# Weight sums of a seven-product mlp by adding DMAs, activation sums and squared ReLU on VectorE

## What is computed

```python
def squared_relu_mlp(xn, w_ff1, w_ff2):
    h = jax.nn.relu(jnp.einsum('bsd,df->bsf', xn, w_ff1))
    return jnp.einsum('bsf,fd->bsd', h * h, w_ff2)
...
        xn = rmsnorm(h, norm_mlp_g[l])
        h = h + squared_relu_mlp(xn, w_ff1[l], w_ff2[l])
    return rmsnorm(h, norm_final_g)
```

## Time and profile before

| | |
|---|---|
| median of 3 runs | 3379.59 us (3378.85 to 3383.29) |
| profiled execution | 3375.55 us, its span 3373.8 us |
| mean granted TensorE clock | 0.965 |
| PE busy over the span | 3018.7 us (89%) |
| VectorE (DVE), ScalarE (ACT), GpSimd (POOL) | 1725.5, 1108.4, 578.7 us |
| DMA | 370.07 MB, mean 110 GB/s |
| mlp | from 2696 to 3364 us of the span |

### The profile page before, as it was taken

The page is one execution under the profiler, slowest core; times in us unless marked ns, Lnnn a source line. Parts: engine busy times, 40 slices in busy tenths (PEclk is TensorE's granted clock), DMA queues, the critical chain, the costliest instruction groups (busy, mean ns, idle before and its releaser), DMA issues. The chain is left out here.

```text
span 3373.8 us, 36498 instructions
## 1 busy us (share of the span) xinstructions
PE 3018.7 (89%) x14456; PEld 2254.7 (67%) x14456; DVE 1725.5 (51%) x2218; ACT 1108.4 (33%) x1640; POOL 578.7 (17%) x375
## 2 busy tenths in 40 slices
PE   7997778999998888877874999999999989999998
PEld 7886754667776575322222877888787767777776
DVE  4126856884444344111114746531215379898988
ACT  3433335663334221100003131121222354636363
POOL 0002022110000001111112000000000055656663
PEclk9998889999999999999997999999999999999999
DMA  3111000003220038999995122211113111111111
GB/s 100 47 48 6 10 14 1 1 1 119 75 81 13 26 143 344 420 421 420 415 414 235 59 67 52 81 50 50 35 55 123 38 63 51 50 51 51 50 57 50
DMA packets 140073, 370.07 MB, mean 110 GB/s; under 512 B 45888, under 2 KB 59840, under 8 KB 113920
## 3 DMA queue, kind: packets, MB, share of 16 engines
q1 hardware_dynamic: 129552, 346.97, 28.3%
q0 software_dynamic: 9216, 16.80, 1.3%
q10 hardware_dynamic: 1152, 4.19, 0.3%
HBM read 352.70 MB, written 32.83 MB: 114 GB/s over the span
## 5 line engine op out<-in xcount | busy, mean ns | idle before, releaser
L4351 PE MATMUL mlp_ps<-mlp_w_ring,mlp_a_ring 128*128 128x512 f32 x1344 | 316.3, 397 | 18.3 <-issue 13.1
L4351 PE MATMUL mlp_ps<-mlp_a_ring,mlp_w_ring 128*128 128x512 f32 x1344 | 313.1, 393 | 21.2 <-issue 13.9
L4285 POOL TENSOR_TENSOR mlp_raw<-mlp_raw 128x1024 f32<-128x1024 f32 x64 | 178.6, 2797 | 892.0 <-POOLq L572 671.0
L4351 PEld LDWEIGHTS mlp_ps<-mlp_w_ring,mlp_a_ring 128*128 128x128 f32 x1344 | 257.9, 193 | 76.1 <-issue 21.9
L4351 PEld LDWEIGHTS mlp_ps<-mlp_a_ring,mlp_w_ring 128*128 128x128 f32 x1344 | 253.0, 189 | 79.0 <-issue 24.1
L517 DVE TENSOR_TENSOR m_w_cut<-m_w_raw,m_w_cut 128x512 fp32r<-128x512 f32 (+1 forms) x86 | 80.8, 940 | 414.0 <-ACT m_w_cut L513 413.6
L2963 PE MATMUL ffn_ps<-moe_wgu,moe_rowsT 128*64 128x512 f32 x1024 | 243.0, 630 | 51.5 <-issue 25.9
L513 ACT ACTIVATE m_w_cut<-m_w_raw 128x512 fp32r<-128x512 f32 (+1 forms) x86 | 71.4, 830 | 490.4 <-PE m_gates_ps L626 190.7
L2999 DVE TENSOR_TENSOR moe_hid<-ffn_ps,moe_gated 128x256 f32<-128x256 f32 x32 | 13.6, 425 | 414.3 <-ACT moe_gated L3011 414.3
L4241 DVE TENSOR_TENSOR mlp_w_ring<-mlp_raw,mlp_w_ring 128x1024 fp32r<-128x1024 f32 x112 | 219.6, 1961 | 0.0
L2963 PEld LDWEIGHTS ffn_ps<-moe_wgu,moe_rowsT 128*64 128x64 f32 x1024 | 78.7, 145 | 195.2 <-issue 166.7
(11 more groups left out here) (575 smaller groups left out, 6457.0 us busy)
## 6 DMA issues: line engine op xcount, KB each, us to landing
moe_wgu<-in_moe_w_gate_dram SPq DMA_DIRECT2D x64, 1024.0 KB, 19.3
moe_wgu<-in_moe_w_up_dram SPq DMA_DIRECT2D x64, 1024.0 KB, 24.6
moe_wd<-in_moe_w_down_dram SPq DMA_DIRECT2D x64, 1024.0 KB, 25.5
mlp_raw<-in_w_ff_dram SPq DMA_DIRECT2D x64, 512.0 KB, 6.5
m_w_raw<-in_w_in_dram SPq DMA_DIRECT2D x48, 256.0 KB, 2.8
mix_w_raw<-in_w_in_dram SPq DMA_DIRECT2D x40, 256.0 KB, 2.6
m_w_raw<-in_w_in_dram SPq DMA_DIRECT2D x20, 512.0 KB, 3.7
x_w_raw<-in_x_w_kv_dram SPq DMA_DIRECT2D x16, 512.0 KB, 3.6
```

The costliest lines, as they stand in the source:

```text
L4285: nc.gpsimd.tensor_tensor(out, l, r, ALU.add if name == "S1" else ALU.subtract).then_inc(self.summed, 1)
L4351: ins = self.nc.tensor.matmul(self.ps[:, 4 * banks + tile], l, r, start=(opens and h == k == n == 0), stop=(h == k == 1 and n == 2), skip_ ...
```

## The change

GpSimd no longer computes. The schemes' signs are turned so that each T is a sum with plus signs only: T1 = B11 + B12, T2 = B22 + B11 + B12, T4 = T2 + B21, T3 = B22 + B12. The products of index 3, 4 and 5 come out negative and are subtracted (or copied with scale -1) when they are taken. B22 is loaded twice, into slots 2 and 3, and 10 DMAs a unit of 512 KB, issued on GpSimd's queue with an add, put the other quarters on top: B11, B12 and later B21 on slot 2, B12 on slot 0 (over B11, when its split is done) and on slot 3. A second set of semaphores (`more`) counts them. The first four of unit 0 are issued in m2_out's block (`tail.gpsimd`), where that block's GpSimd part gets a call. S1 to S4 are VectorE instructions after the low parts of pieces 1, 2, 3, 4, 6 and 7 of the unit. The squared ReLU is one VectorE instruction, max(x, 0) times x, behind the adds of the product that completes the block. ScalarE's two go.

```diff
@@ project: GpSimd's part of the block
                 if side:
                     side.gpsimd(pool)
+                if tail:
+                    tail.gpsimd(pool)
...
+NEGATIVE = (3, 4, 5)
+SUMS = (("S1", 0), ("S2", 0), ("S1", 1), ("S2", 1), ("S4", 0), ("S4", 1), ("S3", 0), ("S3", 1))
+SUMS_AT = {1: SUMS[0:2], 2: SUMS[2:4], 3: SUMS[4:5], 4: SUMS[5:6], 6: SUMS[6:7], 7: SUMS[7:8]}
...
-SLOTS = {"B11": 0, "B21": 1, "B12": 2, "B22": 3, "T1": 0, "T2": 4, "T3": 2, "T4": 4}
+SLOTS = {"B11": (0, 1), "T1": (0, 2), "B21": (1, 1), "T2": (2, 3), "T4": (2, 4), "B22": (3, 1), "T3": (3, 2)}
+MORE = (1, 0, 3, 1)
...
+    def filled(self, eng, u, slot, h, times):
+        if times == 1:
+            eng.wait_ge(self.arrived[slot][h], 16 * (u + 1))
+        else:
+            eng.wait_ge(self.more[slot][h], 16 * (MORE[slot] * u + times - 1))
...
+    def load_more(self, pool, u, name, slot, h):
+        pool.dma_start(self.raw[:, slot, 2 * h:2 * h + 2], self.block_of(u, name, h),
+                       accum_op=ALU.add).then_inc(self.more[slot][h], 16)
@@ high_w
-        if name[0] == "B":
-            act.wait_ge(self.arrived[SLOTS[name]][h], 16 * (u + 1))
-        else:
-            act.wait_ge(self.summed, self.sum_done(u, name, h))
+        self.filled(act, u, SLOTS[name][0], h, SLOTS[name][1])
@@ sum
+    def sum(self, dve, u, name, h):
+        nc, out = self.nc, self.a_sum(name, h)
+        if name == "S1":
...
+            ins = nc.vector.tensor_tensor(out, self.a_block(u, "A22", h), self.a_block(u, "A21", h), ALU.subtract)
+        elif name == "S2":
...
+            ins = nc.vector.scalar_tensor_tensor(out, self.a_sum("S1", h), -1.0, self.a_block(u, "A11", h),
+                                                 ALU.mult, ALU.subtract)
+        elif name == "S4":
+            dve.wait_ge(self.a_low, self.split(u, "S2", h))
+            ins = nc.vector.scalar_tensor_tensor(out, self.a_block(u, "A12", h), -1.0, self.a_sum("S2", h),
+                                                 ALU.mult, ALU.subtract)
         else:
+            dve.wait_ge(self.a_low, self.split(u, "S4", h))
+            ins = nc.vector.tensor_tensor(out, self.a_block(u, "A11", h), self.a_block(u, "A21", h), ALU.subtract)
+        ins.then_inc(self.summed, 1)
@@ take
-                    nc.scalar.activation(at, ps, ACT.Copy).then_inc(self.copied, 1)
+                    nc.scalar.activation(at, ps, ACT.Copy, scale=-1.0 if q in NEGATIVE else 1.0).then_inc(
+                        self.copied, 1)
...
-                nc.vector.tensor_tensor(at, ps, at, ALU.add).then_inc(self.added, 1)
+                nc.vector.tensor_tensor(at, at, ps, ALU.subtract if q in NEGATIVE else ALU.add).then_inc(
+                    self.added, 1)
@@ square
-            act.wait_ge(self.added, self.adds[self.at(u, q)] + 2 * h + 2)
-            self.nc.scalar.activation(at, at, ACT.Relu).then_inc(self.squared, 1)
-            act.wait_ge(self.squared, self.final_done(u, block, h))
-            self.nc.scalar.activation(at, at, ACT.Square).then_inc(self.made, 1)
+            dve.wait_ge(self.added, self.adds[self.at(u, q)] + 2 * h + 2)
+            self.nc.vector.scalar_tensor_tensor(at, at, 0.0, at, ALU.max, ALU.mult).then_inc(self.made, 1)
@@ begin
-        for name in ("B11", "B21", "B12"):
+        for name, slot in (("B22", 2), ("B11", 0), ("B21", 1)):
             for h in range(2):
-                self.load(sp, 0, name, h)
+                self.load(sp, 0, name, slot, h)
+    def first_sums(self, pool, u):
+        for name, times in (("B11", 1), ("B12", 2)):
+            for h in range(2):
+                self.filled(pool, u, 2, h, times)
+                self.load_more(pool, u, name, 2, h)
@@ run, SP
+                        if u == 0:
+                            sp.wait_ge(rows.turned, NT)
                             for h in range(2):
+                                self.load(sp, 0, "B22", 3, h)
+                            continue
+                        for name, slot, was in (("B21", 1, "B21"), ("B11", 0, "T1"), ("B22", 3, "T3"), ("B22", 2, "T4")):
+                            for h in range(2):
+                                sp.wait_ge(self.w_low, self.split(u - 1, was, h))
+                                self.load(sp, u, name, slot, h)
@@ run, GpSimd
                     for u in range(len(units)):
-                        for name, h in SUMS:
-                            self.sum(pool, u, name, h)
+                        if u:
+                            self.first_sums(pool, u)
+                        for name, slot, was in (("B12", 0, "B11"), ("B21", 2, "T2"), ("B12", 3, "B22")):
+                            for h in range(2):
+                                pool.wait_ge(self.w_low, self.split(u, was, h))
+                                self.load_more(pool, u, name, slot, h)
@@ run, VectorE
                         u, q, h = self.piece(g)
+                        for name, half in SUMS_AT.get(2 * q + h, ()):
+                            self.sum(dve, u, name, half)
                         if h:
                             self.take(dve, u, q, "vector")
+                            if units[u].up and any(not first for _, first in TAKES[q]):
+                                self.square(dve, u, q)
...
+    def gpsimd(self, pool):
+        self.sevens.first_sums(pool, 0)
```

More of the change, by code:

```diff
@@ L4140, in __init__ @@
         self.arrived = [[sem(f"slot{s}_half{h}_arrived") for h in range(2)] for s in range(4)]
+        self.more = [[sem(f"slot{s}_half{h}_more") for h in range(2)] for s in range(4)]
         self.a_high, self.a_low, self.w_high, self.w_low = [sem(n) for n in ("a_high", "a_low", "w_high", "w_low")]
-        self.summed, self.products, self.added, self.copied, self.squared, self.made = [sem(n) for n in (
-            "summed", "products", "added", "copied", "squared", "made")]
+        self.summed, self.products, self.added, self.copied, self.made = [sem(n) for n in (
+            "summed", "products", "added", "copied", "made")]
         self.adds, self.copies = [], []
@@ L4190, in c_block, with block_of, load @@
         return self.units[u].dst[:, 4 * i + tile, j * CH:(j + 1) * CH]
-    def load(self, sp, u, name, h):
+    def block_of(self, u, name, h):
         i, k = int(name[2]) - 1, int(name[1]) - 1
-        src = self.units[u].w[:, 4 * k + 2 * h:4 * k + 2 * h + 2, i * CH:(i + 1) * CH]
-        sp.dma_start(self.w_slot(name, h), src).then_inc(self.arrived[SLOTS[name]][h], 16)
+        return self.units[u].w[:, 4 * k + 2 * h:4 * k + 2 * h + 2, i * CH:(i + 1) * CH]
+    def load(self, sp, u, name, slot, h):
+        sp.dma_start(self.raw[:, slot, 2 * h:2 * h + 2], self.block_of(u, name, h)).then_inc(
+            self.arrived[slot][h], 16)
+    def load_more(self, pool, u, name, slot, h):
+        pool.dma_start(self.raw[:, slot, 2 * h:2 * h + 2], self.block_of(u, name, h),
+                       accum_op=ALU.add).then_inc(self.more[slot][h], 16)
     def act_ready(self, eng, u, name, h):
@@ new lines, in sum @@
+    def sum(self, dve, u, name, h):
+        nc, out = self.nc, self.a_sum(name, h)
+        if name == "S1":
+            self.act_ready(dve, u, "A22", h)
+            self.act_ready(dve, u, "A21", h)
+            if u:
+                dve.wait_ge(self.a_low, self.split(u - 1, "S1", h))
+            ins = nc.vector.tensor_tensor(out, self.a_block(u, "A22", h), self.a_block(u, "A21", h), ALU.subtract)
+        elif name == "S2":
+            if u:
+                dve.wait_ge(self.a_low, self.split(u - 1, "S3", h))
+            dve.wait_ge(self.summed, self.sum_done(u, "S1", h))
+            ins = nc.vector.scalar_tensor_tensor(out, self.a_sum("S1", h), -1.0, self.a_block(u, "A11", h),
+                                                 ALU.mult, ALU.subtract)
@@ L4277, in sum @@
         elif name == "S4":
-            mine("S2")
-            pool.wait_ge(self.a_low, self.split(u, "S2", h))
-            l, r = self.a_block(u, "A12", h), self.a_sum("S2", h)
-        else:
-            mine("S4")
-            pool.wait_ge(self.a_low, self.split(u, "S4", h))
-            l, r = self.a_block(u, "A11", h), self.a_block(u, "A21", h)
-        nc.gpsimd.tensor_tensor(out, l, r, ALU.add if name == "S1" else ALU.subtract).then_inc(self.summed, 1)
+            dve.wait_ge(self.a_low, self.split(u, "S2", h))
@@ L4371, in _ @@
                     for u in range(len(units)):
-                        if u:
+                        if u == 0:
+                            sp.wait_ge(rows.turned, NT)
                             for h in range(2):
-                                sp.wait_ge(self.w_low, self.split(u - 1, "T1", h))
-                                self.load(sp, u, "B11", h)
+                                self.load(sp, 0, "B22", 3, h)
+                            continue
+                        for name, slot, was in (("B21", 1, "B21"), ("B11", 0, "T1"), ("B22", 3, "T3"), ("B22", 2, "T4")):
                             for h in range(2):
```

(19 more changed lines are left out.)

39 lines of the change are left out of this document (4 added, 35 removed).

## The result

The kernel after takes 3339.32 us, the median of 4 runs (3335.91 to 3343.0); the kernel before took 3380.41 beside it (3378.85 to 3383.29). The ratio is 0.9878, 95% interval 0.9861 to 0.9895: faster by 1.2%, where 3335 us was forecast and 3328 to 3364 was the range. The profiled execution took 3335.98 us, its span 3334.2.

What follows compares the result with a forecast made beforehand. TensorE, with holes made by GpSimd's sums, was taken as the bound. The profiled 3375.55 - 49.2 (mlp) + 5 (m2_out) gave 3331.3; with the profiled run 4.0 below the median, the forecast was 3335 us, range 3328 to 3364.

Steps and rivals of the forecast that it cites:

- Unit 0, units 1 to 6, unit 7: In the mlp's eight units, closing TensorE's holes was to gain 14.2, 27.3 and 7.7 us, together 49.2 us.
- What makes the holes: In the mlp, GpSimd's sums delay themselves and VectorE's splits: subtractions take 3.42 us beside a sum, against 1.22 alone.
- VectorE's spacing: In each mlp unit, subtractions 1.14 us apart, VectorE about 61 of 76 us; low parts done +5.6 us, needed at +10.9.
- The adding DMA's landing: In the mlp, each adding DMA of weights was to land in 10 us, between 3.2 and about 20.
- the T2 chain: Before piece 4 of a unit, two adding DMAs in a row; each may take 14 us, beyond that 2 us per us.
- Traffic: Per mlp unit, loads take 28 of 76 us at a plain load's price, an estimated 45 at half rate; covered.
- Issuing: On POOL in the mlp, 1.05 to 4 us per adding DMA; slowing of VectorE taken as zero, 2.2 us at most.
- m2_out: Before the mlp, the first four adding DMAs meet a full queue and lengthen TensorE's hole: 0 to 10 us, 5 taken.
- Somewhat late sums: At piece 4, adding DMAs landing in 14 to 17 us cause 0 to 44 us of waits: 3335 to 3375; chance 0.12.
- slow adding DMAs: At piece 4, landings from 17 us make the kernel slower than before, 3419 us at 20 us; chance 0.14.
- VectorE held up by POOL's issues: In the mlp, ten DMA issues per unit at 2.2 us each add 7 us in eight units: 3391 us; chance 0.03.
- holes that don't close: In the mlp, another wait, an add that frees a bank, stands behind the holes: half the gain, 3360 us; chance 0.03.

## Why the prediction was right

**What bounds.** Right: TensorE, with holes. The balance is 620.6 us for the mlp against a forecast of 619, and VectorE 497 against 490 to 510. The 619 rests on counted, unbroken units and repeats. The gain of 49.2 is that of one trace of the kernel before: the other trace of the same mlp code (664.3 us) would have given 3.9 less.

**Unit 0, units 1 to 6, unit 7.** Unit 0 takes 82.9 us (2704.28 to 2787.18) against a forecast of 83.1, units 1 to 6 76.16 each, and unit 7 80.7 where 76.2 + 2.54 stood. Of the 2.0 us too many there, 1.6 are in the last 48 matmuls, 12.76 us where the kernel before had 11.13: the forecast kept the hole before them and left out the clock behind it.

**What makes the holes.** Right that it is GpSimd's sums, by lateness and by slowing VectorE. The text did not say which sums. Taking away those of weights alone gives 43.4 of 47.5 us, those of activations alone 20.7. The squares were priced at "only the 0.6 us hole before piece 12", 2.4 us over four units; they are worth 3.5, and only with the adding DMAs there. Without them the same edit costs 27 us.

**VectorE's spacing.** The low parts end at +5.4 us of the unit, +5.6 in the text. A squared ReLU takes 1.22 us, 1.28 in the text.

**The adding DMA's landing.** Taken as 10 between 3.2 and 20; it is 6.3 at the median and 12.3 at most, in m2_out's full queue. It never reached the 14 us of the T2 chain. The margin was no guess: the run that shortened it brought the holes in the place named.

**Traffic.** The rows gave 28 of 76 us; the share of 0.57 is 43, near the 45 estimated by the rule of the Trainium skill (Collectives: The Full Stack, "The bandwidth ceiling"). Neither moves the mlp, but it does move m2_out.

**Issuing.** 1.20 us on POOL, within 1.05 to 4, and VectorE's subtractions beside them stayed at 1.22: taken as zero, and so it is.

**m2_out.** 5 taken in a range of 0 to 10; 6.4 measured. The hole grew by 4.7 (2.88 to 7.57) and the granted clock of 0.76 in the 8 us behind it took another 8 x 0.24 = 1.9. The mechanism was as described. The text had 2.7 us of traffic for two DMAs at a plain one's price and 5.4 at twice that; the hole grew by 2.3 (to 5.15) in the run with plain ones and by 4.7 with adding ones. Then comes the slow clock. In the run with plain ones it took more (granted 0.64 in the 8 us behind the hole), so m2_out was only 1.5 us shorter there. How much of the 6.4 is the adding itself is thus known only roughly. That the 5 came near was luck in part: it was a pick from the middle of a wide range.

**The sum.** 3375.55 - 49.2 + 5 = 3331.3, measured 3335.98: 1.6 from the last hole's clock, 1.4 from m2_out, and 1.6 from the later start of m2_out, which no part of the change explains and which lies within the scatter of the traces.

**The rivals.** Somewhat late sums, slow adding DMAs, VectorE held up by POOL's issues and holes that don't close: none came.

## What to carry to other kernels

A sum of two tensors that both come from DRAM can be made by the transfer itself; here it costs the DMA engines twice a plain load and GpSimd 1.20 us to issue, and no tensor instruction, and it pays most where the engine that did it also slows the one that feeds TensorE. Before such a change, count the slack of the slot that takes the most additions in a row, and look for the place where its first DMAs meet a full queue. Three parts that come in one edit may each have another sign alone: try them in combination, and not only by taking one away.

## What was not expected of the hardware

- An adding DMA of 512 KB has 272 packets against 144, and the same bytes in the profile's count; GB/s alone shows a queue that seems to have room (247 GB/s at a share of 1.06, where plain loads moved 387 at 1.03), so the share is the column to read.
- A VectorE scalar_tensor_tensor whose two SBUF inputs are the same tensor is slowed by GpSimd's sums too: 4.66 us for two, against 2.36. The Trainium skill (SBUF — State Buffer, "Who interferes with whom") says that an instruction with two SBUF inputs contends with one of GpSimd that reads SBUF; these rows agree. Issuing DMAs on POOL does not do it here.
- A hole costs clock or not, and not by its length alone. Behind 2.72 us in m2_out the clock stayed 1.00; behind 5.15 and 7.57 it was 0.64 and 0.76 for 8 us. Behind the 3.3 us hole before piece 8 it was 1.00, 0.82 and 0.62 in three units of one trace. The hole of 2.53 before the last 48 matmuls cost 1.6 us more in the kernel after (12.76, 12.77 and 12.67 in three traces) than in the one before (11.13 and 11.16). What decides was not tested.
